# Expert stage of a hybrid encoder step: blocks of 32 rows on four column tiles, and down by turns with the next block's gate and up

## What is computed

```python
D_MODEL, N_EXPERTS, TOP_K, D_FF = 1024, 32, 4, 1024
def moe(x2, w_router, b_router, w_gu, b_gu, w_dn, b_dn):
    logits = (x2 @ w_router) + b_router
    top_v, top_i = lax.top_k(logits, TOP_K)
    gates = jax.nn.softmax(top_v, axis=-1)
    ...
    def expert_block(args):
        xb, e = args
        gu = xb @ w_gu[e] + b_gu[e]
        gate = jnp.minimum(gu[:, :D_FF], SWIGLU_LIMIT)
        up = jnp.clip(gu[:, D_FF:], -SWIGLU_LIMIT, SWIGLU_LIMIT)
        hid = (up + 1.0) * gate * jax.nn.sigmoid(SWIGLU_ALPHA * gate)
        return hid @ w_dn[e] + b_dn[e]
    ...
    return jnp.zeros_like(x2).at[stok].add(ys[dest] * sgate[:, None])
```

## Time and profile before

| | us |
|---|---|
| median of 3 runs | 2022.53 |
| lowest and highest | 2017.26, 2026.97 |
| the profiled execution | 2029.72 |
| its span | 2028.1 |

### The profile page before, as it was taken

How to read it: one execution, slowest core, us unless ns; L and a number is a source line. 1 busy time by engine, 2 the same in 40 slices (tenths; PEclk the granted TensorE clock), 3 DMA queues, 4 the chain that set the end, 5 groups by cost and what they waited for, 6 DMA issues and landing times.

```text
span 2028.1 us, 20268 instructions
## 1 busy us (share of the span) xinstructions
PE 1713.7 (84%) x7096; PEld 785.5 (39%) x7097; DVE 372.9 (18%) x899; ACT 337.1 (17%) x695; POOL 116.8 (6%) x220
## 2 busy tenths in 40 slices
PE   2999988688889999499788899887889987899890
PEld 1666654355556664333222233222233322233230
DVE  1272033322220011511101111011011110111113
ACT  1141254211211000111111111110111111111111
POOL 0021000000000000110000000000000000000002
PEclk9998976766767999689998999999999999999995
DMA  9387300101012352479999898999988999859894
GB/s 295 129 238 229 107 22 0 34 0 42 0 42 83 125 188 101 169 287 407 404 411 403 331 400 336 404 404 409 407 324 337 403 403 412 335 208 405 325 384 140
DMA packets 115540, 511.29 MB, mean 252 GB/s; under 512 B 11601, under 2 KB 15422, under 8 KB 82606
## 3 DMA queue, kind: packets, MB, share of 16 engines
q1 hardware_dynamic: 98862, 454.98, 57.0%
q0 software_dynamic: 16640, 55.81, 9.4%
HBM read 471.21 MB, written 39.55 MB: 252 GB/s over the span
## 4 chain that ended last, share of the span: by engine, by line
PE 62%; DMA 22%; DVE 6%; SPq 4%; ACT 3%; issue 2%; POOL 0%; DVEq 0%; ACTq 0%; POOLq 0%
PE bank L505 31%; DMA ring<-in_w_gate_up 21%; PE bank L835 11%; PE bank L863 8%; PE bank L843 8%; PE bank L509 3%; PE bank L824 2%; DVE r_c L1129 1%; SPq L484 1%; ACT ring L890 1%; SPq L488 1%; DVE r_kv L1123 1%; ACT r_kv L890 1%; DMA bgu<-in_b_gate_up 1%; SPq L423 0%
## 5 line engine op out<-in xcount | busy, mean ns | idle before, releaser
L835 PE MATMUL bank<-ring,r_kv 128*64 128x512 f32 x1872 | 421.1, 596 | 35.7 <-DMA ring<-in_w_gate_up 35.3
L863 PE MATMUL bank<-ring,r_kv 128*64 128x512 f32 x1248 | 276.4, 595 | 26.8 <-ACT r_kv L890 26.8
L505 PE MATMUL bank<-r_xt,ring 128*128 128x336 f32 (+2 forms) x896 | 258.8, 452 | 1.1 <-DVE r_xt L1126 1.1
L835 PEld LDWEIGHTS bank<-ring,r_kv 128*64 128x64 f32 x1872 | 128.9, 137 | 321.9 <-issue 227.6
L1123 DVE TENSOR_SCALAR r_kv<-bank 128x512 f32<-128x512 f32 (+1 forms) x80 | 55.0, 687 | 1000.1 <-PE bank L843 977.6
L843 PE MATMUL bank<-ring,r_kv 128*64 128x512 f32 x624 | 165.4, 679 | 53.5 <-DMA ring<-in_w_gate_up 53.5
L505 PEld LDWEIGHTS bank<-r_xt,ring 128*128 128x128 f32 (+2 forms) x896 | 167.2, 187 | 91.1 <-issue 12.3
L863 PEld LDWEIGHTS bank<-ring,r_kv 128*64 128x64 f32 x1248 | 86.1, 137 | 192.0 <-issue 155.9
L843 PEld LDWEIGHTS bank<-ring,r_kv 128*64 128x64 f32 x624 | 53.4, 155 | 161.3 <-issue 161.2
L1082 ACT ACTIVATE r_o<-r_kv 128x512 f32<-128x512 f32 x39 | 24.6, 630 | 538.4 <-DVE r_kv L1123 538.4
L505 PE MATMUL bank<-ring 64*128 64x257 f32 (+4 forms) x208 | 78.9, 528 | 22.6 <-DVE r_qk L1126 11.1
(11 more groups left out here) (213 smaller groups left out, 1121.2 us busy)
## 6 DMA issues: line engine op xcount, KB each, us to landing
ring<-in_w_gate_up SPq DMA_DIRECT2D x256, 1024.0 KB, 19.9
ring<-in_w_down SPq DMA_DIRECT2D x128, 1024.0 KB, 22.6
ring<-in_w_in SPq DMA_DIRECT2D x12, 2048.0 KB, 7.8
r_v<-x_rows POOLq DMA_DIRECT2D x41, 256.0 KB, 7.2
y_rows<-r_xt POOLq DMA_DIRECT2D x78, 128.0 KB, 5.4
x_rows<-r_c POOLq DMA_DIRECT2D x7, 1024.0 KB, 21.5
x_rows<-r_c POOLq DMA_DIRECT2D x9, 768.0 KB, 19.5
y_rows<-r_c POOLq DMA_DIRECT2D x1, 5376.0 KB, 33.3
```

The costliest lines, as they stand in the source:

```text
L505: ins = pe.matmul(out, l, r, start=(n == 0), stop=(n == len(pairs) - 1), **kw)
L835: ins = pe.matmul(half(gate_bank if q < 2 else up_bank, q % 2), xg[:, k, :], w[:, 512 * q:512 * q + 512], start=False, stop=False, skip_gr ...
L863: ins = pe.matmul(half(out_bank, t), hidT[:, j, BLK * h:BLK * h + BLK], w[:, h, 512 * t:512 * t + 512], start=(j == 0 and h == 0), stop=(j ...
```

## The change

Blocks have 32 rows (`BLK` = 32), and all buffers of a block are half as wide. A matmul has 32 stationary columns and 256 streaming ones, and gate, up and the output each lie in four column tiles of 32 partitions and 256 columns of their bank. There are twice as many matmul instructions in a block, each with half the columns.

TensorE's loop is written anew. The first block's gate and up stand ahead of it. A turn of the loop then does block b from the hidden values on, and gate and up of block b + 1: its biases, k-tiles 0 and 1, the turns of block b's hidden values, then down 0, k-tiles 2 and 3, down 1, k-tiles 4 and 5, down 2 and 3, and k-tiles 6 and 7. The last block's down stands behind the loop. GpSimd stores the output in four pieces instead of two. SyncE's order and its waits stay. `MAXB`, the greatest number of blocks, goes from 53 to 74 and with it the tables' width; `x_rows` has 2432 rows instead of 3520.

```diff
-NE, TOPK, BLK = 32, 4, 64
+NE, TOPK, BLK = 32, 4, 32
...
-        xg = r3(r_kv[:, 0:512], 8)
-        hidT = r3(r_kv[:, 512:1024], 4)
+        xg = r3(r_kv[:, 0:256], 8)
+        hidT = r3(r_kv[:, 512:768], 2)
...
-            def half(bank, t):
-                return bank[BLK * t:BLK * t + BLK, :]
+            def tile(bank, t):
+                return bank[BLK * t:BLK * t + BLK, 0:256]
...
+                for q in range(8):
+                    pe.matmul(tile(gate_bank if q < 4 else up_bank, q % 4), pick[:, q // 2, :],
+                              bgu[:, 256 * (q % 2):256 * (q % 2) + 256], start=True, stop=False, skip_group_check=True)
+
+            def gate_up(k, e):
+
+                pe.wait_ge(up_in[k], 16 * e + 16)
+                w = up_w(k)
+                for q in range(8):
+                    ins = pe.matmul(tile(gate_bank if q < 4 else up_bank, q % 4), xg[:, k, :],
+                                    w[:, 256 * q:256 * q + 256], start=False, stop=False, skip_group_check=True)
+                ins.then_inc(m_up, 1)
...
+            def hidden_turned(b):
+
+                pe.wait_ge(m_hid, b + 1)
+                for j in range(2):
+                    ins = turn(ht_bank[:, 128 * j:128 * j + 128], hid[:, 128 * j:128 * j + 128])
+                ins.then_inc(m_turn, 1)
+
+            def down(j, e):
+
+                pe.wait_ge(dn_in[j], 16 * e + 16)
+                w = dn_w(j)
+                for h in range(2):
+                    s = 2 * h + j // 2
+                    for t in range(4):
+                        ins = pe.matmul(tile(out_bank, t), hidT[:, j % 2, BLK * s:BLK * s + BLK],
+                                        w[:, h, 256 * t:256 * t + 256], start=(j == 0 and h == 0),
+                                        stop=(j == 3 and h == 1), skip_group_check=True)
+                ins.then_inc(m_down, 1)
...
+            for k in range(6):
+                gate_up(k, 0)
+            gate_up_end(0)
+            last = pe.snap(nb - 1)
+            with pe.Fori(0, last) as b:
...
+                bias(b + 1)
+                pe.wait_ge(m_xg, b + 2)
+                gate_up(0, e1)
+                gate_up(1, e1)
+                hidden_turned(b)
                 pe.wait_ge(m_hidT, b + 1)
                 pe.wait_ge(yrow_free, b + 1)
...
+                for j in range(2):
+                    down(j, e)
+                    gate_up(2 * j + 2, e1)
+                    gate_up(2 * j + 3, e1)
+                down(2, e)
+                down(3, e)
+                gate_up_end(e1)
...
-                for h in range(2):
-                    pool.dma_start(dst[:, 512 * h:512 * h + 512], yrow[BLK * h:BLK * h + BLK, :]).then_inc(m_store, 16)
-                pool.wait_ge(m_store, 32 * b + 32)
+                for h in range(4):
+                    pool.dma_start(dst[:, 256 * h:256 * h + 256], yrow[BLK * h:BLK * h + BLK, :]).then_inc(m_store, 16)
+                pool.wait_ge(m_store, 64 * b + 64)
```

More of the change, by code:

```diff
@@ L815, in _ @@
             tokens_turned()
-            def half(bank, t):
-                return bank[BLK * t:BLK * t + BLK, :]
+            def tile(bank, t):
+                return bank[BLK * t:BLK * t + BLK, 0:256]
             def bias(b):
                 pe.wait_ge(m_pick, b + 1)
-                for q in range(4):
-                    pe.matmul(half(gate_bank if q < 2 else up_bank, q % 2), pick[:, q, :], bgu[:, :],
-                              start=True, stop=False, skip_group_check=True)
-            bias(0)
@@ L828, in _ @@
-            with pe.Fori(0, nb) as b:
-                e = pe.value_load(bei[0:1, bass.ds(b, 1)].bitcast(I32), min_val=0, max_val=NE - 1)
-                pe.wait_ge(m_xg, b + 1)
-                for k in range(6):
-                    pe.wait_ge(up_in[k], 16 * e + 16)
-                    w = up_w(k)
-                    for q in range(4):
-                        ins = pe.matmul(half(gate_bank if q < 2 else up_bank, q % 2), xg[:, k, :],
-                                        w[:, 512 * q:512 * q + 512], start=False, stop=False, skip_group_check=True)
-                    ins.then_inc(m_up, 1)
+                for q in range(8):
+                    pe.matmul(tile(gate_bank if q < 4 else up_bank, q % 4), pick[:, q // 2, :],
+                              bgu[:, 256 * (q % 2):256 * (q % 2) + 256], start=True, stop=False, skip_group_check=True)
@@ L841, in _ @@
                     for k in (6, 7):
-                        for t in range(2):
-                            ins = pe.matmul(half(bank_, t), xg[:, k, :],
-                                            up_w(k)[:, 512 * (q0 + t):512 * (q0 + t) + 512], start=False,
+                        for t in range(4):
+                            ins = pe.matmul(tile(bank_, t), xg[:, k, :],
+                                            up_w(k)[:, 256 * (q0 + t):256 * (q0 + t) + 256], start=False,
                                             stop=(k == 7), skip_group_check=True)
@@ L1075, in tokens @@
             def tokens():
-                return copy(xg[:, :, :], banks[0][:, :].rearrange("p (k s) -> p k s", k=8))
+                return copy(xg[:, :, :], banks[0][:, 0:256].rearrange("p (k s) -> p k s", k=8))
             act.wait_ge(m_gath, 1)
```

49 lines of the change are left out of this document (25 added, 24 removed).

## The result

| | before | the change |
|---|---|---|
| median, us | 2026.97 (19 runs) | 2032.74 (19 runs) |
| lowest and highest | 2017.26, 2032.21 | 2027.99, 2043.11 |
| profiled execution, us | 2029.72 | 2033.26 |
| its span | 2028.1 | 2031.7 |

The change takes 1.0042 of the time before (95% interval 1.0025 to 1.0058): +5.8 us between the medians, where +5.2 was forecast; the ratio with its interval is +5 to +12 us. So the time is right; its terms are not all, as the profile shows.

A forecast was written before the change was run, and what follows sets the result against it. The prediction took DMA's 404 GB/s ceiling plus six silences, 76.5 us, to bound the expert stage. Block rows -13, stores +3, silences +7.5, start 0 and end +7.7 gave +5.2: 2028 us, range 2008 to 2085.

The forecast's parts named there:

- Part 1: Expert matmuls: four column tiles overlap fully, four records in 0.215 us, so a k-tile takes 0.86 us, formerly 1.72.
- Both rivals by which they overlap less: Column tiles: partial overlap, period 15.8 us, 2061 us total, chance 0.14; only two at once, 24.0, 2152, chance 0.13.
- the four steps of the bias: Earlier trace: the bias's 8 records end in 1.94 us, four steps, where strict program order would need five, 2.36 us.
- Part 2, the block rows: Block row traffic on the software queue: 20.16 MB falls to 15.2, -13 us; smaller store pieces cost +3 us.
- Part 3, the interleave: TensorE's expert loop: dense block period 12.9 us for 24.9; silences of the DMA engines 84.0 us against 76.5, +7.5.
- six first slots: In the six silences, the first weight slot of an expert's second block was forecast free at 4.2 us.
- eight middle periods: Middle blocks of experts with three or five blocks: each us of period costs 8 us; forecast period 12.9 us.
- 84.0: Forecast sum of DMA silences in us: five of 9.7 at three-block experts, one of 35.5 at the five-block expert.
- the 2 us for the clock: Added to each forecast DMA silence, because TensorE's clock is lower after waits.
- the +10: Sum past which the change counts as slower; with only two tiles at once, passed from a period of about 13.5 us.
- cost 0: SyncE's unchanged load order: enough loads stay queued while down waits for landings, so DMA doesn't run dry; 0 us.
- The end: After the last weight landing: last expert's two blocks let down end 11.8 us later, +6.6, store issues +1.1; together +7.7.

The follow-up runs named there:

- e6: The change with each column tile's gate and up matmuls written in a row in k-tiles 0 to 5; 2034.85 us in one execution.
- e15: The change with one register load at the head of TensorE's loop instead of two; median 2043.15 us, 1.0119 of the kernel before.
- e16: The change with one register load at TensorE's loop head and down waiting for the output bank instead of the row buffer; 2024.06 us, 0.9999 of before.
- e10: The change with TensorE's down waiting for the output bank, and ScalarE waiting for the row buffer instead; 2035.9 us, 1.0067 of before.
- e2: The change's new order of TensorE's work, but with the 64-row blocks and two column tiles of the kernel before; 2068.86 us, 1.0238 of before.
- e9: The change with four register loads at the head of TensorE's loop instead of two; 2070.1 us in one execution.

## Why the prediction was right, step by step

**Part 1 held.** Four column tiles overlap in full: 16 records in 0.86 us, two down pieces in 1.73 (1768.51 to 1770.24), the bias in 0.89. Both rivals by which they overlap less are out, and e6 shows what I could only infer from the four steps of the bias: a second record of one tile doesn't hold up the other tiles. The rule of the Trainium skill ("TensorE: Matmul & The Clock Gate", Packing small matmuls), matmuls in strict program order, does not hold for these streams: by it e6 would have taken about 2.8 us a k-tile.

**Part 2, the block rows, was mis-sized.** I priced the traffic saved at the mean rate, 2.5 us a MB, and added 3 us for smaller pieces: -10. The earlier trace rows had the right price, 62.3 us for 20.16 MB, 3.1 a MB. The change shows 4.1% x 1089.0 = 44.6 us for 14.81 MB: -17.7. (The 13 us itself is 12.3 by the 20.16 and 15.2 MB that it names.) The weights' own share fell from 973.7 to 968.1 us, for which I have no reason. Together -23, and the rest shrank by 21.7.

**Part 3, the interleave: right mechanism, period too short.** I forecast 12.9 us; it is 13.8. The largest missing term is the loop's head, 0.67 of the 0.9 us: two register loads of 0.64 us each, with too little queued ahead of them. The other 0.24 are spread over the other steps; e15, without the idle time, still has 13.17. The longer period enters each of the six first slots (6 x 0.66 = 4.0) and eight middle periods (8 x 0.9 = 7.2). 84.0 + 4.0 + 7.2 = 95.2; measured 95.1. e15, without that idle time, checks the same sum: 84.0 + 8 x 0.27 = 86.2; measured 86.2. Such a fit is in part luck, since the 2 us for the clock are in it: e16 has the same period and 79.3 us. By these two terms, 11.2 us, the longer period alone would have moved the forecast from +5 to +16 us, which is past the +10 from which the prediction calls it slower. In the change the 2 us a silence for the clock was right on average (with the period of 13.81 us the sum without it is 83.2, and 95.1 were measured) and not one by one: this stands at the start of the silence of 13.6 us.

```profile
1885.85 1.38 PE L862 MATMUL bank<-ring,r_kv 128*32 128x256 f32 x16 [2.26 <-POOLq L1573]
1886.98 3.35 PE L832 MATMUL bank<-ring,r_kv 128*32 128x256 f32 x32
```

A wait of 2.26 us for the row buffer, and behind it two k-tiles at a lower clock, 3.35 us for 1.91, with a granted clock of 0.54 from 1887.0 to 1890.1 us. That the buffer comes 2 us late under load, and that it costs nothing there, was forecast; e10's total bears it out. Just ahead of a silence it can cost all the same: this one is 12.9 us in e15, with a wait of 2.85 us for the buffer ahead of it and two k-tiles of 3.42 us behind it, and 9.0 us in e16, without the wait and with k-tiles of 1.92. That SyncE's order costs nothing (cost 0) held in the change, by the 407 GB/s outside its silences. In e2, at 64 rows, the same order costs about 50 us; that the slack of TensorE with 32 rows makes the difference is argued.

**The end was too cheap.** TensorE ends 14.2 us after the last landing (5.2 before), forecast 11.8:

```profile
1970.70 1.92 PE L843 MATMUL bank<-ring,r_kv 128*32 128x256 f32 x32
...
1974.41 0.44 PE L509 MATMUL bank<-const,r_v 128*128 128x128 f32 x2 [1.20 <-DVE r_v L1164]
1975.57 5.15 PE L862 MATMUL bank<-ring,r_kv 128*32 128x256 f32 x64 [0.71 <-ACT r_kv L925]
...
1981.82 2.24 POOL L1571 DMA_DIRECT2D y_rows<-r_xt  x4 [4.74 <-ACT r_xt L925]
...
1986.54 1.06 POOL L1581 DMA_INDIRECT ring<-y_rows,r_qk  x1 [0.55 <-POOL u_pad L1577]
```

Gate and up end 6.1 us after the landing instead of 4.2 (the longer period, and a wait before), the pause is 2.9 instead of 3.9, and after two idle stretches the last down takes 5.15 us instead of 3.7. From down's end to the gather it is 5.8 us with four stores, and was 5.6 with two (1979.84 to 1985.46), not the 1.1 more that I had put for them. From the end of the last output store's issue to the end of the span it is 7.4 us and was 4.4, which may be chance. 9.0 + 0.2 + 3.0, and 0.5 less in between: +11.7 against +7.7.

**Sum.** Forecast -10 + 7.5 + 0 + 7.7 = +5.2. Measured in the two profiles: rest -21.7, silences +17.8, start -4.3, end +11.7: +3.5, with the start being chance. The two errors of about 11 us, rest and silences, are independent and cancel; the total is better than its terms deserve.

## What to carry to other kernels

Where every buffer is in use and the consumer has little slack, the order in which the loads are issued must be the order in which the reworked consumer frees the buffers; a second queue did not replace that here. Price traffic by its queue's share of the engines, not by the mean rate. When matmul streams get shorter, look for what the sequencer does between them: it was covered before, and now its idle time shows up, with four register loads also in the clock.

## What the runs showed of the hardware

- Four column tiles of 32 with 256 f32 columns run at once, 0.215 us for four records, whether the tiles are written by turns or each twice in a row.
- A register load on TensorE costs 0.64 us of its sequencer; one was hidden at the loop's head, the second was not (0, 0.67 and 1.95 us of idle time with one, two and four).
- Behind two of three pauses of 1.95 to 1.98 us in the long silence of e9 the granted clock was 0.55 and 0.60 in the next k-tiles (3.25 and 2.98 us for 1.91); behind those of 0.67 us in the change's long silence it was 1.00.
- One store of 128 partitions whose DRAM side has an outer dimension of 4 ran on four engines and landed in 7.4 us; four stores of 32 partitions landed in 4.7 each.
